# A hybrid decoder step: the gather ring runs on over stage boundaries, and expert tokens and rows are spread anew over the stages

## The reference

```python
def peer(x, w_q, keys, u_tab, v_tab):          # x: 128 tokens at a time, 1024 wide
    q = x @ w_q ; s = q . keys                  # 8 heads x 2 halves x 128 keys
    sv, si = top_k(s, 16); cand = sv0 + sv1     # 16 x 16 candidates a head
    cv, ci = top_k(cand, 16); idx = i1 * 128 + i2   # 16 experts a head, 128 a token
    gate = softmax(cv)
    act = gelu(einsum('thkd,td->thk', u_tab[idx], x))
    return einsum('thk,thkd->td', gate * act, v_tab[idx])
```

## Time and profile before

| | us |
| --- | --- |
| median of 3 runs | 5030.12 |
| the runs | 5026.23 to 5057.6 |
| the profiled execution, its span from the first to the last instruction | 5061.9 |
| of it P0, M0 | 257.5, 301.4 |
| M1, P2, M2, M3, M4 | 386.2, 386.8, 335.2, 399.1, 442.0 |
| P5, M5, M6, M7, M8 | 483.9, 330.9, 396.3, 431.2, 644.8 |
| `experts_folded`, `store_states` | 260.3, 6.3 |

### The profile page before, as it was taken

How to read it: one execution, slowest core, us unless ns; L and a number is a source line. 1 busy time by engine, 2 the same in 40 slices (tenths; PEclk the granted TensorE clock), 3 DMA queues, 4 the chain that set the end, 5 groups by cost and what they waited for, 6 DMA issues and landing times. The chain is left out here.

```text
span 5061.9 us, 53189 instructions
## 1 busy us (share of the span) xinstructions
PE 3427.8 (68%) x17745; PEld 1968.4 (39%) x17745; DVE 3195.1 (63%) x7030; ACT 725.4 (14%) x2596; POOL 2650.2 (52%) x2240
## 2 busy tenths in 40 slices
PE   7978377599887576556579988757656564565516
PEld 5666262255462452343144446245234322321101
DVE  5335896588544896677668744489667755664370
ACT  2141110111210210210022121021021011000000
POOL 1000376465435575676546533557567647726564
PEclk9988668699888678776789999877877776677659
DMA  5453478899859789989879875978999988879897
GB/s 180 145 192 119 175 262 327 295 368 353 322 181 366 268 314 369 336 320 335 336 271 355 307 293 167 369 275 307 368 344 321 367 317 300 303 295 361 300 370 281
DMA packets 460478, 1497.56 MB, mean 296 GB/s; under 512 B 53184, under 2 KB 115456, under 8 KB 447632
## 3 DMA queue, kind: packets, MB, share of 16 engines
q0 software_dynamic: 317952, 1141.01, 61.7%
q1 hardware_dynamic: 121040, 330.55, 17.6%
q10 hardware_dynamic: 21216, 22.60, 1.4%
HBM read 1455.22 MB, written 55.52 MB: 298 GB/s over the span
## 5 line engine op out<-in xcount | busy, mean ns | idle before, releaser
L2122 POOL DMA_INDIRECT e_ring<-peer_u,e_idx x1024 | 1325.0, 1294 | 647.9 <-issue 231.6
L2122 POOL DMA_INDIRECT e_ring<-peer_v,e_idxT x1024 | 1119.7, 1093 | 891.4 <-PE e_ff L2274 445.5
L2158 DVE CUSTOM_DVE_ANT_0 e_ring<-e_ring,e_x 128x1024 f32<-128x1024 f32 x1024 | 1226.5, 1234 | 291.1 <-DMA e_ring<-peer_u,e_idx 270.6
L2274 PE MATMUL e_ff<-e_ring,e_strips 128*32 128x512 f32 x4096 | 672.4, 786 | 512.0 <-DMA e_ring<-peer_v,e_idxT 429.5
L352 PE MATMUL p_ps<-p_hT,p_w 128*128 128x256 f32 (+2 forms) x1728 | 569.9, 484 | 0.0
L2274 PEld LDWEIGHTS e_ff<-e_ring,e_strips 128*32 128x32 f32 x4096 | 146.5, 129 | 933.9 <-issue 931.7
L352 PEld LDWEIGHTS p_ps<-p_hT,p_w 128*128 128x128 f32 x1728 | 329.0, 195 | 209.0 <-issue 129.5
L1138 POOL CAST hidden<-delta 128x128 bf16<-128x128 f32 (+1 forms) x9 | 2.9, 317 | 629.7 <-DMA delta<-hidden 605.7
L376 PE MATMUL p_ps<-p_w,p_hT 128*128 128x512 f32 (+1 forms) x576 | 251.2, 599 | 0.0
L1299 PE MATMUL bank<-X,atp 128*128 128x128 f32 (+1 forms) x1120 | 170.5, 304 | 102.3 <-DVE XT L1736 70.7
L1313 PE MATMUL bank<-T,XT 128*128 128x128 f32 (+1 forms) x1088 | 167.8, 304 | 93.1 <-DVE T L1744 91.4
(11 more groups left out here) (392 smaller groups left out, 5150.1 us busy)
## 6 DMA issues: line engine op xcount, KB each, us to landing
p_w<-w_in SPq DMA_DIRECT2D x156, 512.0 KB, 3.6
wbuf<-wc SPq DMA_DIRECT2D x56, 1024.0 KB
wbuf<-w_out SPq DMA_DIRECT2D x40, 1024.0 KB
e_ring<-peer_v,e_idxT POOLq DMA_INDIRECT x1104
atp<-w_out SPq DMA_DIRECT2D x16, 1024.0 KB
kb_kdec<-w_out SPq DMA_DIRECT2D x16, 1024.0 KB
atp<-wc SPq DMA_DIRECT2D x16, 1024.0 KB
e_ring<-peer_u,e_idx POOLq DMA_INDIRECT x1024
```

The lines of the kernel that those rows point to most:

```text
L2122: g.indirect_dma_start(out=self.ring[:, i % RING, :], out_offset=None, in_=table[:, :], in_offset=at, bounds_check=NEXP - 1, oob_is_err=Fa ...
L2158: v.tensor_tensor_reduce(out=self.ring[0:U, i, :], in0=self.ring[0:U, i, :], in1=self.x[0:U, :], scale=1.0, scalar=0.0, op0=ALU.mult, op1= ...
L2274: last = nc.tensor.matmul(self.ff[i][32 * j:32 * j + 32, :], self.strips[:, self.strip_of[t] % NSTRIP, j, 31 - s:63 - s], self.ring[:, sel ...
```

## The change

The counts by stage, as u rows / v tokens of a tail / v tokens of a head (the same total of 1024 u rows and 1024 v tokens; `experts_folded` keeps its own):

| stage | before | after |
| --- | --- | --- |
| M1 | 128 / 0 / 80 | 128 / 0 / 80 |
| P2 | 128 / 48 / 0 | 64 / 48 / 0 |
| M2 | 0 / 0 / 128 | 64 / 0 / 112 |
| M3 | 128 / 0 / 80 | 128 / 16 / 64 |
| M4 | 128 / 48 / 64 | 128 / 64 / 32 |
| P5 | 128 / 64 / 0 | 64 / 96 / 0 |
| M5 | 0 / 0 / 128 | 64 / 0 / 112 |
| M6 | 128 / 0 / 80 | 128 / 16 / 64 |
| M7 | 128 / 48 / 64 | 128 / 64 / 48 |
| M8 | 128 / 64 / 128 | 128 / 80 / 128 |

In M2 and M5 the 64 u rows lie in the first half of the inverses, and the turn stands between the halves (`early`). The y of tiles 1 and 4 moves from the end of M2 and M5 to the middle of M3 and M6. In projection stages the first tail tokens are used between the transposes of the layer norm (`"ln", i`), in mix stages at `start`, ahead of the wait for the stage's rows. The ring keeps its place and its counts over the stages. `pool_end` no longer waits for landings and doesn't reset the queue; it gathers the next stage's first entries, up to 12 (`fresh`): first those with known indices (`known`), then u rows behind `taken`. By the weights that is, as known / behind `taken`: M0 0 / 12, M1 8 / 2, P2 12 / 0, M2 4 / 8, M3 12 / 0, M4 12 / 0, P5 12 / 0, M5 4 / 8, M6 12 / 0, M7 12 / 0. ACT's `Exp` now stands ahead of the strips of the last `best` point. The diff, cut to its core:

```diff
+    w = {}
+    for i in range(len(tiles)):
+        w["ln", i] = (4, 0, 0)
+    w["ln"] = (0, 2, 0)
...
         g.memset(self.e.ring[:, 0:9, :], 0.0).then_inc(self.S["k_clear"], 1)
         g.wait_ge(self.S["k_clear"], 1)
+        g.wait_ge(self.S["taken"], 4)
+        for i in range(self.then.fresh()):
+            self.e.gather(g, self.S, self.then, i)
...
+    "rest": {"start": (0, 0, 0), "norm": (0, 0, 0), "prep": (0, 6, 0), "raw": (0, 8, 0), "inv0": (0, 6, 0), "T": (0, 3, 0),
+             "X": (0, 3, 0), "r": (0, 2, 0), "o": (0, 4, 0), "raw2": (0, 0, 4), "inv02": (0, 0, 4), "T2": (0, 0, 0.8),
...
-    "series": {"start": (0, 0, 0), "norm": (0, 0, 0), "prep": (0, 2, 0), "raw": (3, 4, 0), "inv0": (3, 3, 0), "T": (1.6, 2, 0),
+    "series": {"start": (14, 0, 0), "norm": (0, 0, 0), "prep": (0, 2, 0), "raw": (3, 4, 0), "inv0": (3, 3, 0), "T": (1.6, 2, 0),
...
+                        if hf == 1 and s == 1 and peer.plan.early:
+                            pe.wait_ge(S["w_taken"], 1)
...
                     at("o", hf)
+                    if hf == 0 and peer.plan.early:
+                        peer.tensor_turn(pe, bank[5])
...
-                for e in range(EH):
+                for e in range(EH - 1):
                     at("best", e)
                 act.wait_ge(S["soft"], 1)
                 nc.scalar.activation(B["best"][0:R], B["best"][0:R], ACT.Exp).then_inc(S["exp_ready"], 1)
+                at("best", EH - 1)
                 peer.scalar_end(act)
...
+    def known(self):
+        n = 0
+        while n < min(RING, len(self.seq)) and (self.seq[n][0] == "v" and (self.seq[n][1] < self.n_tail or not self.U) or
+                                                self.seq[n][0] == "u" and not self.starts):
+            n += 1
+        return n
+    def fresh(self):
+        n = self.known()
+        while n < min(RING, len(self.seq)) and self.seq[n][0] == "u":
+            n += 1
+        return n
...
     def pool_end(self, g):
+        S, p, then = self.S, self.plan, self.then
         self.pool_at()
-        S = self.S
-        for i in range(RING):
-            if self.landings[i]:
-                g.wait_ge(S[f"in{i}"], 16 * self.landings[i])
-        g.sem_inc(S["gathered"], 1)
-        nums = [S[f"in{i}"].num for i in range(RING)]
-        g.dma_reset(range(min(nums), max(nums) + 1))
+        if then is None:
+            return
+        for i in range(then.fresh()):
+            if i == then.known():
+                g.wait_ge(S["taken"], 4)
+            if len(p.seq) + i >= RING:
+                self.freed(g, len(p.seq) + i - RING)
+            self.gather(g, S, then, i)
...
     def take_choice(self, v):
         S = self.S
-        v.wait_ge(S["gathered"], 1)
         self.copy_choice(v, S)
         v.wait_ge(S["taken"], 4)
...
+            (1, dict(u=(0, 0, SLOTS), head=(0, 0, 80))),
+            ([2, 3, 4], dict(tail=(0, 80, P), u=(1, 0, 64))),
+            (2, dict(u=(1, 64, SLOTS), head=(1, 0, 112), early=True)),
+            (3, dict(tail=(1, 112, P), u=(2, 0, SLOTS), head=(2, 0, 64))),
+            (4, dict(tail=(2, 64, P), u=(3, 0, SLOTS), head=(3, 0, 32))),
+            ([5, 6, 7, LAST], dict(tail=(3, 32, P), u=(4, 0, 64))),
+            (5, dict(u=(4, 64, SLOTS), head=(4, 0, 112), early=True)),
+            (6, dict(tail=(4, 112, P), u=(5, 0, SLOTS), head=(5, 0, 64))),
+            (7, dict(tail=(5, 64, P), u=(6, 0, SLOTS), head=(6, 0, 48))),
+            (LAST, dict(tail=(6, 48, P), u=(7, 0, SLOTS), head=(7, 0, P)))]
```

More of the change, by code:

```diff
@@ L288, in _ @@
                 ident = B["ident"]
-                if peer:
+                if peer and peer.plan.starts:
                     peer.tensor_start(pe, ps[5])
@@ L679, with __init__ @@
     names = ["k_keys", "k_wq0", "k_wq1", "k_wq2", "k_comb", "k_evac", "k_wc0", "k_wc1", "k_clear", "taken"]
[L681 to L684, removed]
+    def __init__(self, io, e, then):
+        self.io, self.e, self.then, self.plan = io, e, then, Plan(checkpoint_weights("rows"), u=(0, 0, SLOTS))
+        self.upto = dict(self.plan.upto)
+        self.plan.starts = self.plan.turns = self.plan.early = False
     def begin(self, nc, ctx, S):
-        self.nc, self.S, self.U = nc, S, 0
+        self.nc, self.S = nc, S
     def steps(self, emit):
@@ L1481, in _ @@
                 at("turn")
-                if peer.U:
+                if peer.plan.turns and not peer.plan.early:
                     peer.tensor_turn(pe, bank[3])
@@ L1602, in _ @@
                     at("o", hf)
+                    if hf == 0 and peer.plan.early:
+                        peer.scalar_turn(act, bank[5])
                 b = U.ready(act, "BCT")
@@ L1803, in _ @@
                     at("o", hf)
+                    if hf == 0 and peer.plan.early:
+                        peer.vector_turn(v)
                 U.taken(v, "PD", 1)
@@ L2497, in experts_folded @@
         nc.all_engine_barrier(sems_to_clear=S.range)
+        nums = [x.num for x in pool_dma.values()]
+        nc.all_engine_barrier(sems_to_clear=range(min(nums), max(nums) + 1))
 def store_states(nc, io, B):
@@ new lines, in program @@
+        plans, base, counts = [], 0, [0] * RING
+        for some, parts in stages:
+            mixed = None if isinstance(some, list) else some
+            points = project_points(some) if mixed is None else checkpoint_weights("rest" if "early" in parts else "series")
+            plans.append(Plan(points, base, counts, mixed=mixed, **parts))
+            plans[-1].sent = plans[-1].fresh()
+            base, counts = base + len(plans[-1].seq), plans[-1].counts
+        project(nc, io, B, [0, 1], pool_dma, consts=Constants(io, B, e))
@@ L2542, in program @@
+        e.bind(io, B, None, None)
+        mix_tile(nc, io, B, pool_dma, 0, Keys(io, e, plans[0]))
+        for (some, _), plan, then in zip(stages, plans, plans[1:] + [None]):
+            e.bind(io, B, plan, then)
+            if plan.mixed is None:
+                project(nc, io, B, some, pool_dma, peer=e)
+            else:
+                mix_tile(nc, io, B, pool_dma, plan.mixed, e)
+        experts_folded(nc, e, pool_dma, base, counts)
         store_states(nc, io, B)
```

277 lines of the change are left out of this document (139 added, 138 removed).

## The result

The changed kernel takes 5247.2 us (median of 4 runs, 5241.8 to 5255.7) against 5029.5 (4 runs): the ratio is 1.0419, 95% interval 1.0391 to 1.0446, slower by some 211 us. I had forecast slower by 80, a median of 5110 us in a range of 4960 to 5160. The profiled execution has a span of 5245.5 us, 183.6 more than that of before, whose own profile lay 0.6% above its median.

The account below looks back on a forecast made before the run. No single bound: PE paces P2, DVE M3's inverses, DMA much of M4's. Terms 104 + 12.6 + 29 - 24 - 16 - 27 + 1 gave +80 us, 5030 to 5110; range 4960 to 5160.

Parts of the forecast that it names:

- (e): M3 and M6: 12 more tail tokens, y in the middle, fewer head tokens and earlier Exp; -8 us each, -16.
- (f): M4 and M7: fewer head tokens, 16 more tail tokens each; -17 us in M4, -10 in M7, sum -27.
- (c): Other stage boundaries: POOL's last issues delay the barrier, leftover gathers share DMA with the next loads; +29 us.
- Rival 3: POOL can't fill the ring ahead of the barrier, gathers only delay loads, M2's turn makes PE wait; 5150 us, chance 0.1.
- (b): M0 to M1: 12 u-row issues ahead of the barrier cost 15.6 us, M1 gains about 3; +12.6 us.
- (a): 64 u rows into the first half of M2's and M5's inverses, with the turn; +52 us each, +104.
- (d): P2 and P5 lose 64 u rows each, but PE keeps its pace; -15 us and -9, sum -24.
- rival 1: DMA sets the pace, filled holes win time; P2's blocks under 5.43 us, stage over 30 shorter; 4931 us, chance 0.2.
- Rival 2: Prices near the gentle bounds: M2 and M5 +35 us each, boundaries 0, P -35; total +5, 5035 us, chance 0.2.

Follow-up runs that it names:

- old_counts_ahead: The changed kernel with u rows and tokens per stage as before, the ring still running on by up to 12 gathers; ratio 1.0132 to before.
- tails_only: The changed kernel with u rows per stage as before and only the new token placement, M2's and M5's y included; ratio 1.0237 to before.
- no_drain: The changed kernel with projection and mix stages closed by a barrier of semaphores alone, so POOL has no drain; ratio 1.0284 to before.
- before_exp: The kernel before with only ACT's Exp moved ahead of the strips of the last best point; ratio 0.9997 to before.
- half_split: The changed kernel with 96 u rows in P2 and P5 and 32 in M2 and M5; ratio 1.0256 to before.
- thin_gathers: The changed kernel with M2's and M5's u-row gathers of 64 elements in place of 1024, dots unchanged; ratio 1.0442 to before.
- cheap_dots: The changed kernel with dots of M2's and M5's u rows over 64 of 1024 columns, gathers unchanged; ratio 1.0384 to before.
- thin_both: The changed kernel with both gathers and dots of M2's and M5's u rows over 64 elements in place of 1024; ratio 1.0391 to before.

## Why the prediction was wrong

Slower was right; 80 us was 211, and the median of 5247 lies above the range. By the runs the 211 are 66 for the ring (old_counts_ahead, which also has the earlier `Exp` and the tokens at the start), 53 for the tokens (tails_only) and 92 for the split on top of both; the split alone costs 138. My terms for the same three were 43, -43 and 80. The largest miss is the tokens, steps (e) and (f), where I booked a gain that isn't there. The one in mechanism is the ring, step (c), where I took gathers in flight for free.

- **(c), "POOL's 12 hide there" and the last four issues alone being in the way: failed.** I counted issues, 1.30 us each, and took gathers in flight for free. POOL's drain waits until they have landed. From the last reduction to the barrier M1, M3 and M6 pay 20 to 21 us more than before, where I had 4 to 5. The stages grew by less, since that reduction comes earlier in them. In P2 and P5 the drain ends long before PE, as I had it, and M8, which begins with 12 gathers ready, came out 15 us shorter where I had +7. "DMA busy over each boundary" was wrong for the change (0.00 for 5.1 us) and right for no_drain. Rival 3 had the right place and another reason: POOL could fill the ring, but the barrier waited for the landings.
- **(b): the same.** M0's last reduction comes 297.0 us into the stage, the barrier at 321.1, 24.1 us where it was 2.4; 15.6 were issues. M1 reaches its last reduction 10 us earlier, which its own drain takes back.
- **(f), "13 x 1.41 = 18, of which 15 count": failed.** In M4's stretch up to the candidates 7 issues less stand, not 13, and it takes 154.1 us for the 153.0 of before: the tokens taken from there gave nothing back. So gathers don't set that stretch, though DMA shows 0.90 to 0.94 in it; what does was not isolated. Its end took 1.7 us more for my -6. The inverses are 6.1 us longer than before for my 4, but that is luck: the ring alone had made them 16 us shorter (186.9 in old_counts_ahead for 203.3), and the tokens took that back. M4 and M7 moved +5.4 and +12.5 for -15 and -6.
- **(e), "the earlier Exp and 8 tokens less give -14": failed.** The reduction did move by that much (41.7 us in after for 56.4), but the end belongs to the last landings; before_exp moved nothing. The inverses took 13.9 us more for my 6, of which 11.2 are the wait behind the four tail tokens, and the stretch behind gave 9.2.
- **(a): the main sub-term was too small.** I halved the 115.3 us of the inverses, but the first half has 48.7. So DVE had 23.3 us idle there and not 30.7, and my own sum would have given 41 in place of 34; the half pays 42.5. That this sum comes out is in part luck: for the 32 rows of half_split it gives 4, and 13.2 were paid. The reason I gave isn't the whole either: with DVE's dots nearly gone the half stayed, and "DMA needs 90 us ... so it hides" left out that POOL takes up to 2 us an issue beside u rows. The turn and the tokens behind it cost 6.6 us for my 10. Ahead of the inverses it is +1.3, behind them +7.7 for my 5; the reduction comes 6.6 us earlier for my 7, and the end is 17.7 us longer for my 10.4, by the drain. +69 for 52.
- **(d): the pace was right.** P2's blocks and the window that answers to the earlier trace rows:

```profile
1084.01 5.43 PE L356 MATMUL p_ps<-p_hT,p_w 128*128 128x384 f32 x16
```

```profile
1027.00:1242.00 215.00, 201.39 (x775) 113.09 (x773) 149.09 (x288) 43.36 (x145) 76.78 (x71) 0.98 0.83 279
```

DMA fell from 0.98 to 0.83, PE is busy 201 of 215 us as before, a block is 5.43 us. So rival 1's condition isn't met, and its gain from the boundaries isn't there even without the drain. P2 is 10 us shorter than in old_counts_ahead, for my 15, and the ring gives 8 of them back at P2's start and end. Rival 2's gentle bounds were on the wrong side of every term but M8's.

What stays open: where in M4 to M7 the 53 us of tails_only fall (single profiles scatter by as much); what holds M2's first half at 93 us once the dots are cheap; and whether a turn with PE's part placed later in the second half would cost less, which wasn't tried.

## What to carry to other kernels

Before letting transfers of POOL's queue run over the end of a block, look for the drain there and price it as issue plus landing, or close the block with semaphores alone; then ask whether the idle DMA time at the boundary was in anyone's way. When work moves into a stretch with idle time on one engine, count all engines that the work passes (here POOL's issues, DMA and DVE), with the price that a step has beside the others and not alone. Cut two versions at the same events before you compare parts of them; half of a stretch isn't its first half. A wait that ends early is a gain only if nothing else ends at the same time: read what stands behind it before booking it.

## What the runs showed of the hardware

- A drain in POOL's queue at the end of a block waits for the indexed gathers that POOL has issued: its row lasts 7 to 16 us with gathers in flight, 5.5 to 9.7 of them behind the end of the last issue, and 0.03 with none. With rows of 256 bytes in place of 4096 it lasted 5.0 us behind the last issue in place of 18.7 (end of P2, thin_gathers and after). In M1 it ended 5 us after DMA had fallen silent (0.00 from 969.4 to 974.5), so it costs more than the transfer. The Trainium skill (VectorE: DVE Perf Modes, The DRAIN you can't avoid) tells DVE's flush from drains of some 12 ns that all engines have as boilerplate; POOL's here, 13.9 us in the median, is neither, and the measurement decides.
- An indexed gather of 128 rows costs POOL 1.30 us per issue whether a row has 4096 bytes (cheap_dots) or 256 (thin_both, DMA at 0.22). Beside DVE's products of 128 x 1024 it costs up to 2.3, again with both: 49 gathers had POOL busy 75.2 us in after, 47 had it busy 74.3 in thin_gathers, and 56 only 56.5 in cheap_dots.
